# Reordering the middle of a hybrid mixer on Trainium2: the rope sum ahead of Pool's second level, score maxima and predicated copies taken in another order

## The reference

```python
y_hy = hyena_mixer(hy_in, ...)     # two gated long convolutions through a Fourier transform, then a norm
y_mla = mla_mixer(cq, ckv, kr, ...)  # four-head attention over 256 keys, q and k with a rope part
y_gla = gla_mixer(q, k, v, ...)    # gated linear attention, both directions, with decays
x = x + jnp.concatenate([y_hy, y_mla, y_gla], axis=-1) @ w_out

# hyena_mixer, the core
z = x1 * fft_long_conv(v, kern[:, 0], skip[0])
y = x2 * fft_long_conv(z, kern[:, 1], skip[1])
return rms_norm(y.astype(dtype), out_norm)

# mla_mixer, the core, for 128 queries at a time
s = jnp.einsum('bqhd,bkhd->bhqk', q_blk, k).astype(jnp.float32) * scale
p = jax.nn.softmax(s, axis=-1).astype(v.dtype)
return jnp.einsum('bhqk,bkhe->bqhe', p, v)
```

## Time and profile before

| | |
|---|---|
| median of 3 runs | 1030.2 us (1030.1 to 1030.58) |
| profiled execution | 1030.28 us |
| its span, first to last instruction | 1028.3 us |
| TensorE busy | 1001.0 us |
| VectorE, ScalarE, Pool busy | 694.3, 537.3, 110.9 us |
| granted TensorE clock, mean | 0.996 of full speed |

### The profile page before, as it was taken

How to read it: one execution, slowest core, us unless ns; L and a number is a source line. 1 busy time by engine, 2 the same in 40 slices (tenths; PEclk the granted TensorE clock), 3 DMA queues, 4 the chain that set the end, 5 groups by cost and what they waited for, 6 DMA issues and landing times.

```text
span 1028.3 us, 14899 instructions
## 1 busy us (share of the span) xinstructions
PE 1001.0 (97%) x5596; PEld 846.5 (82%) x5596; DVE 694.3 (68%) x826; ACT 537.3 (52%) x752; POOL 110.9 (11%) x160
## 2 busy tenths in 40 slices
PE   6999999999899999999999999999998999999997
PEld 5888888888777888888878888887886888888886
DVE  5766656676886666566677665657579776656665
ACT  6554545456654555454465454545466555545453
POOL 2000000150431200000020000003315220000001
PEclk9999999999999999999999999999999999999999
DMA  8466454444303564545455545452542235554551
GB/s 292 170 241 227 165 204 163 164 167 149 136 13 152 177 233 163 204 163 204 165 199 184 225 163 204 163 204 90 198 168 78 83 141 207 184 204 164 203 184 42
DMA packets 27080, 175.85 MB, mean 171 GB/s; under 512 B 3200, under 2 KB 3712, under 8 KB 6560
## 3 DMA queue, kind: packets, MB, share of 16 engines
q1 hardware_dynamic: 25744, 172.90, 45.8%
q0 software_dynamic: 720, 1.95, 0.8%
q10 hardware_dynamic: 576, 0.45, 0.1%
HBM read 174.58 MB, written 1.05 MB: 171 GB/s over the span
## 4 chain that ended last, share of the span: by engine, by line
issue 50%; PE 38%; POOL 9%; DVE 1%; DMA 1%; ACT 1%; POOLq 1%; SPq 0%; ACTq 0%; DVEq 0%
PE psum L1070 16%; PE psum L1071 8%; PE psum L1064 5%; PE psum L1066 4%; PE psum L1065 4%; POOL mixer_scratch L352 3%; POOL mixer_scratch L373 1%; POOL mixer_scratch L372 1%; DMA w_raw<-in_w_dram 1%; POOL statistics L325 1%; POOL statistics L323 1%; POOL x_normed L377 0%; POOL statistics L336 0%; ACT xT_split L430 0%; POOL statistics L339 0%
## 5 line engine op out<-in xcount | busy, mean ns | idle before, releaser
L1070 PE MATMUL psum<-xT_split,w_high 128*128 128x512 f32 x1408 | 501.6, 400 | 4.2 <-DVE w_low L702 2.4
L698 DVE TENSOR_TENSOR w_low<-w_raw,w_high 128x2048 fp32r<-128x2048 f32 (+1 forms) x160 | 362.8, 2270 | 134.4 <-ACT w_high L411 134.4
L1071 PE MATMUL psum<-xT_split,w_low 128*128 128x256 f32 x1408 | 395.6, 281 | 0.0
L1070 PEld LDWEIGHTS psum<-xT_split,w_high 128*128 128x128 f32 x1408 | 265.0, 188 | 72.9 <-issue 6.9
L411 ACT ACTIVATE w_high<-w_raw 128x2048 fp32r<-128x2048 f32 (+1 forms) x160 | 299.7, 1875 | 42.1 <-PE psum L1066 41.5
L1071 PEld LDWEIGHTS psum<-xT_split,w_low 128*128 128x128 f32 x1408 | 266.6, 189 | 1.4
L1064 PE MATMUL psum<-w_high,hT_high 128*128 128x512 f32 (+1 forms) x360 | 140.5, 390 | 0.0
L462 ACT ACTIVATE mixer_scratch<-psum 128x512 f32<-128x512 f32 x88 | 52.5, 596 | 167.4 <-PE psum L1071 167.4
L1066 PE MATMUL psum<-w_high,hT_low 128*128 128x512 f32 (+1 forms) x360 | 139.9, 389 | 0.0
L1065 PE MATMUL psum<-w_low,hT_high 128*128 128x512 f32 (+1 forms) x360 | 139.5, 387 | 0.0
L466 ACT ACTIVATE silu_gate<-hidden 128x256 f32<-128x256 f32 x88 | 36.8, 418 | 135.4 <-DVE hidden L727 135.4
(11 more groups left out here) (187 smaller groups left out, 989.3 us busy)
## 6 DMA issues: line engine op xcount, KB each, us to landing
w_raw<-in_w_dram SPq DMA_DIRECT2D x160, 1024.0 KB, 4.8
w_raw<-in_w_dram SPq DMA_DIRECT2D x8, 256.0 KB, 8.1
x<-in_x_dram SPq DMA_DIRECT2D x2, 512.0 KB, 5.2
mixer_scratch<-in_fil_dram POOLq DMA_DIRECT2D x2, 512.0 KB, 6.1
out_dram<-x_normed SPq DMA_DIRECT2D x3, 256.0 KB, 2.1
mixer_scratch<-in_fil_dram POOLq DMA_DIRECT2D x2, 352.0 KB, 6.1
mixer_scratch<-in_fin_dram SPq DMA_DIRECT2D x1, 512.0 KB, 5.4
dft<-in_dft_dram SPq DMA_DIRECT2D x1, 256.0 KB, 5.1
```

Of the source, the lines that this page charges most:

```text
L698: e.tensor_tensor(filled(WL[p], n), filled(raw[p], n), filled(WH[p], n).bitcast(F32), ALU.subtract).then_inc(s_lo.sem, 1)
L1070: e.matmul(out, ah, XB[:, k, :, :], start=k == 0, stop=False)
L1071: return e.matmul(out[:, 0:SEQ], al, XH[:, k, :], start=False, stop=k == KD - 1)
```

## The change

On Pool the rope sum goes ahead of level 1. On TensorE the first hyena inverse goes ahead of the rotated part of the query, the second hyena transform ahead of the transposes of the rotated query (with a wait for the rope products, because the transform writes the bank that they read), and two heads of the second block's scores ahead of the second hyena inverse, so that all scores are made before the first probabilities are transposed. On VectorE the first spectrum is combined and folded ahead of two weight splits and a level, `gated(l, 0, 0)` goes ahead of the rope products, `level_qk(3)` ahead of the second `gated`, both maxima one place later against the predicated copies, and two keeps one place earlier against a `level_qk`. On ScalarE the copies of QN go ahead of that of KN and a level, one split goes behind two copies, and the scaling of the hyena output is done here instead of on VectorE. The number of matmuls, their shapes and all transfers stay.

```diff
@@ Pool
                 levels(l, 0)
-                levels(l, 1)
                 e.wait_ge(a_qt.sem, a_qt.at(l))
                 e.tensor_tensor(xn[:, :, 768:1024], PE_[:, 0:2, :], PE_[:, 2:4, :], ALU.add).then_inc(a_qr.sem, 1)
+                levels(l, 1)
                 levels(l, 2)
@@ ScalarE
                 values_out(1)
+                e.wait_ge(s_used.sem, used(l, S_UQN))
+                for n in range(2):
+                    copy(QN[:, 2 * n:2 * n + 2, :].rearrange("p a b -> p (a b)"), PS[:, 2 + n, :], a_qn)
                 e.wait_ge(a_km.sem, a_km.at(l))
                 copy(KN[:, 0:2, :].rearrange("p a b -> p (a b)"), PS[:, 4, :], a_kn)
                 level_exp(l, 1)
-                e.wait_ge(s_used.sem, used(l, S_UQN))
-                for n in range(2):
-                    copy(QN[:, 2 * n:2 * n + 2, :].rearrange("p a b -> p (a b)"), PS[:, 2 + n, :], a_qn)
                 e.wait_ge(a_vm.sem, a_vm.at(l))
                 copy(VM[:, 0, :], PS[:, 5, :], a_v)
                 copy(VM[:, 1, :], PS[:, 6, :], a_v)
+                spectrum_odd(l, 1, 7)
                 e.wait_ge(a_qtr.sem, a_qtr.at(l))
                 copy(QR.rearrange("p a b -> p (a b)"), PS[:, 2, :], a_qre)
-                spectrum_odd(l, 1, 7)
-                hi(l, S_WO + 1)
                 e.wait_ge(s_used.sem, used(l, S_UKV))
                 copy(KN[:, 2:4, :].rearrange("p a b -> p (a b)"), PS[:, 1, :], a_kn)
+                hi(l, S_WO + 1)
                 level_exp(l, 2)
@@ ScalarE
                 probs_turned(l, 0)
+                e.wait_ge(h_r.sem, h_r.at(l))
+                for t in range(T):
+                    v = xn[:, t, 0:256]
+                    r = e.activation(v, v, ACT.Copy, scale=st[:, T_RH + t:T_RH + t + 1])
+                r.then_inc(h_yy.sem, 1)
                 level_exp(l, 6)
                 probs(l, 1)
@@ VectorE
                 multiply(l, 0)
-                lo(l, S_UQR)
-                level_qk(l, 0)
-                lo(l, S_UKV)
                 combine(l)
                 fold(l)
+                lo(l, S_UQR)
+                lo(l, S_UKV)
+                level_qk(l, 0)
+                gated(l, 0, 0)
@@ VectorE, behind the rope products
-                gated(l, 0, 0)
                 lo(l, S_WO)
                 level_qk(l, 1)
...
                 level_keep(l, 0)
+                level_qk(l, 3)
                 gated(l, 1, 6)
-                level_qk(l, 3)
+                level_keep(l, 1)
                 score_max(l, 0)
-                level_keep(l, 1)
+                level_keep(l, 2)
                 level_qk(l, 4)
-                e.wait_ge(h_r.sem, h_r.at(l))
-                for t in range(T):
-                    v = xn[:, t, 0:256]
-                    r = e.tensor_scalar(v, v, st[:, T_RH + t:T_RH + t + 1], None, ALU.mult)
-                r.then_inc(h_yy.sem, 1)
-                level_keep(l, 2)
+                level_keep(l, 3)
+                score_max(l, 1)
                 level_qk(l, 5)
-                score_max(l, 1)
-                level_keep(l, 3)
+                level_keep(l, 4)
                 attended(l, 0)
-                level_keep(l, 4)
                 turned_low(l, 2, 0, Y_BANKS[0], Y_TILES[0], C_GO, by_parity)
@@ TensorE
                 r.then_inc(s_used.sem, 1)
+                hy_inverse(l, 0, 0).then_inc(h_inv.sem, 1)
                 e.wait_ge(s_lo.sem, s_lo.at(l, S_UQR + 1))
...
                 r.then_inc(a_vm.sem, 1)
-                hy_inverse(l, 0, 0).then_inc(h_inv.sem, 1)
                 e.wait_ge(h_oc.sem, h_oc.at(l, 1))
                 keys((2, 3)).then_inc(s_used.sem, 1)
+                e.wait_ge(a_qt.sem, a_qt.at(l))
+                e.wait_ge(a_v.sem, a_v.at(l, 2))
+                e.wait_ge(h_z.sem, h_z.at(l, 1))
+                hy_dft(l, 1, 6)
                 e.wait_ge(a_qr.sem, a_qr.at(l))
...
                 r.then_inc(a_qtr.sem, 1)
-                e.wait_ge(a_v.sem, a_v.at(l, 2))
-                e.wait_ge(h_z.sem, h_z.at(l, 1))
-                hy_dft(l, 1, 6)
@@ TensorE
                 scores(l, 0, (3,)).then_inc(a_s.sem, 1)
+                e.wait_ge(h_oc.sem, h_oc.at(l, 2))
+                scores(l, 1, (2, 3))
                 hy_inverse(l, 1, 6).then_inc(h_inv.sem, 1)
                 level_scores(l, 1)
                 e.wait_ge(h_z.sem, h_z.at(l, 2))
-                scores(l, 1, (0, 1, 2))
+                scores(l, 1, (0, 1)).then_inc(a_s.sem, 1)
                 level_scores(l, 2)
                 turn_probs(l, 0)
-                scores(l, 1, (3,)).then_inc(a_s.sem, 1)
                 level_scores(l, 3)
                 attend(l, 0)
```

## The result

| | before | after |
|---|---|---|
| median | 1030.34 us (1030.1 to 1030.58, 5 runs) | 1035.91 us (1035.2 to 1038.16, 5 runs) |
| profiled execution | 1030.28 us, span 1028.3 | 1038.16 us, span 1036.1 |
| mean granted clock of TensorE | 0.996 | 0.992 |

The ratio is 1.0057, 95% interval 1.0046 to 1.0068: slower by 5.6 us at the median, where 3.5 were forecast. The direction and the chain of Part 4 came as predicted, and falls of TensorE's clock, which the prediction held as a rival, came on top of them. The profiled execution is the slowest of the five.

What follows compares the result with a forecast made beforehand. TensorE, busy 97% of the span, bounds the kernel, so only its waits or work count. Two layers at +1.77 us add 3.5 to the profiled 1030.28, giving 1033.8 us; range 1031.3 to 1036.4.

Steps and rivals of the forecast that it cites:

- Part 4: VectorE's second maximum behind the fourth predicated copy, which waits for level 3's scores: second transposes of probabilities +1.77 us per layer.
- Part 1: Rope sum and first hyena inverse: TensorE's wait of 1.11 goes, waits of 0.5 and 0.7 replace it; gain nothing.
- Part 2: Second hyena inverse: its 1.55 wait behind the fold goes; a gain of 2.0 us per layer up to there.
- Part 3: First maximum, now after level 1's keep: TensorE waits 2.1 for the first probabilities, leaving 0.65 of the 2.0 gained.
- Edits at nothing: Hyena scaling on ScalarE, reordered copies, SyncE's fetches and Pool's levels 1 and 2: all covered by waits, costing nothing.
- the clock rival: TensorE's clock falls in sparse stretches of the middle; one or two falls give 1035.0 to 1037.1, likeliest 1036; chance 0.18.
- The row of 9 to 13: Evidence for a clock fall: TensorE busy 1.55 of 4.00 us there, granted clock 0.50 in the next 3.3 us.
- the serial row's 5%: Allowance on some twelve serial durations, 15 us, from inverse to second transposes: 0.75 either way, +1.0 to +2.5 per layer.
- a late rope sum: Worst case on Pool: the sum waits for a 3.27 split, ends at 273.9, and costs 0.4 more after slack.

Runs made afterwards that it cites:

- e8: Changed kernel with VectorE's 2048-column split of the output weights moved behind level 1's product: 1034.69 us, a single execution.
- e2: Changed kernel with the second block's maximum and the sixth level's product ahead of the fourth predicated copy again: 1031.79 us.
- e1: Changed kernel with two groups of 12 dummy transposes per layer where TensorE would wait, level 2's scores ahead of the last two heads: 1034.55 us.
- e6: Changed kernel with the hyena output scaled on VectorE again, plus the same 24 dummy transposes per layer as e1: 1034.42 us.
- e3: Kernel before the change, with only the fourth predicated copy moved ahead of the sixth level's product and the second maximum on VectorE: 1038.61 us.
- e10: e7 with the 2048-column split behind level 1's product, level 7's exponential earlier and the second attention scaling ahead of level 7's product: 1027.26 us.
- e7: An order of the study's own: first block's scores, maximum and probabilities ahead of the second hyena inverse, other queues reordered to match: 1031.85 us.
- e5: e2's order plus the first twelve dummy transposes per layer of e1: 1030.17 us.

## Why the prediction was right, and what it left out

- **Part 1** held in its sum. The transform waited 0.51 (0.5 forecast) and the scores 0.78 for the copy of QR (0.7 forecast); they started at 274.71 without the 0.19, 0.25 later than forecast, 0.17 of it because the transform started at 271.53 and not at 271.36. One term was mis-sized: the rope sum was taken at 1.26 and took 3.25; it ended ahead of the stated worst end at 273.9. Its length cost nothing, as e8 shows. By the rule quoted from the Trainium skill ("SBUF — State Buffer", section "SBUF: two separate sides"), that the first to start keeps the shared port for its whole instruction, the sum would have ended at 272.9; it ended at 273.12, 272.93 without the 0.19, beside a split that began 0.17 before it. The trace agrees with that rule, and the choice of 1.26 was wrong.
- **Part 2** held: the inverse waits for nothing. It started at 281.92 without the 0.19, against 281.7.
- **Part 3**: wait of 2.1 forecast, 2.05 measured. The transposes started at 289.29 without the 0.19, 0.28 later than forecast, so of the 2.0 won 0.37 were left and not 0.65.
- **Part 4** held in its mechanism and nearly in its size: a wait of 2.3 forecast, 2.51 measured in layer 1, where the clock had not fallen before it. e2 shows the cause, since one moved line removes it; e1 and layer 0 of e8 give its price, 2.0 a layer against 1.77. The difference is the 0.25 of Part 1, carried through the chain.
- **Edits at nothing** held for the scaling at the median: e6 against e1.
- **The step that failed** is the one that set the forecast's granted clock to 1.00 through the middle and gave the clock rival 0.18. The rival's mechanism was right, and it came together with the chain: falls behind both transposes in layer 0 and behind the second in layer 1, 1.2 each, the lower end of its price of 1.2 to 1.65 (0.97 in e2, 0.5 in e8, 2.3 in e3). It counted one or two falls, and the profiled execution had three. Its likeliest time, 1036, is the measured one. The row of 9 to 13 in the earlier trace rows was the nearest to the new stretches and pointed the right way; what was argued against it, that nothing is as empty as the first microseconds, is contradicted by the rows after: 0.69 busy of 3.60 against 1.55 of 4.00.
- The rule of the Trainium skill ("TensorE: Matmul & The Clock Gate", Part 1), a fall only after an idle stretch, would have given the forecast's 1033.8. The runs disagree: the clock fell behind stretches in which TensorE was busy 1.75 of 3.80 us and 2.12 of 4.00.

The median stood inside the range of 1031.3 to 1036.4, and that is partly luck: the range's upper end of 1036.4 was nearly all made of the serial row's 5% and of a late rope sum (1036.1), and 1.4 of the 2.1 us between the forecast and the median was the clock. The profiled execution, with three falls, stood outside.

## What to carry to other kernels

In an in-order queue look at what stands behind each instruction that will wait: the second maximum had its scores complete at 286.8 and ran at 294.0, and one moved line was worth 4 us. Where two orders differ by a few microseconds of waiting, count the stretches that they leave sparse on TensorE as well as the waits, because a wait of 2 to 3 us here cost another 0.5 to 1.4 behind it in some executions, and once 2.3. The order of e10, whose waits are 1.2 at most, showed no fall in its profile. Where a Pool step is on the path, look at what VectorE starts just ahead of it: a two-input split of 2.28 made a sum of 1.29 last 3.24.

## What was not expected of the hardware

The fall of the clock is not a fixed property of an order. The kernel of e7 gave times in two groups, 1031.08 to 1031.85 and 1033.39 to 1033.84, and the changed kernel spread over 3.0 us where e5, whose middle showed no fall, spread over 0.8. A wait of 2.05 was followed by a fall in layer 0 of the changed kernel and by none in layer 1, after the same 1.75 busy of 3.80; one of 3.02 in e3 by none, one of 3.30 by the longest fall of all. So the length of a wait alone doesn't decide it, and what does stays open.

Pool's addition of 128x512 took 1.29 when it had started ahead of VectorE's instructions (e8) and 3.24 to 3.25 when a split of 2.28 had started 0.2 ahead of it. The split's rest (271.98 - 269.87 = 2.11) and the 1.29 together make 3.40, so most of the sum's length was waiting for the other engine. The reverse shows in the row behind the split: the product (L842) that started at 271.90 took 1.76, and it ended 0.54 behind the end of the sum at 273.12.
